# Weight-block differences of the down projection made on GpSimd instead of VectorE

## What is computed

```
hid = conv(h @ w_up)                      # 256 x 11264
gate, up = split(hid)                     # 5632 each
y = (gelu(gate) * up) @ w_down            # 256 x 5632 times 5632 x 2048
```

## Time and profile before

| | before |
|---|---|
| median of 3 runs | 2069.21 us (2067.95 to 2069.44) |
| profiled execution, first to last instruction | 2067.5 us |
| TensorE busy | 2054.3 us, 99% |
| VectorE busy | 1525.8 us, 74% |
| ScalarE busy | 987.2 us, 48% |
| GpSimd busy | 15.5 us, 1% |
| TensorE clock granted | 0.999 of full |

### The profile page before, as it was taken

One profiled execution on the slowest core, in us unless ns is written; L12 is line 12 of the kernel. 1 busy time (PEld: TensorE's weight loads), 2 busy tenths in 40 slices (PEclk: granted clock), 3 DMA queues, 4 the chain that ended last, 5 costly groups with the idle time before them and its releaser, 6 DMA issues.

```text
span 2067.5 us, 26666 instructions
## 1 busy us (share of the span) xinstructions
PE 2054.3 (99%) x10852; PEld 1763.2 (85%) x10852; DVE 1525.8 (74%) x1855; ACT 987.2 (48%) x986; POOL 15.5 (1%) x33
## 2 busy tenths in 40 slices
PE   9999999999999999999999999999999999999999
PEld 7888888888888888878888888888887888888887
DVE  5776786444556767678988887888886778888776
ACT  6444363354434455465544544455454434444642
POOL 0000000000000000000000000000000000000000
PEclk9999999999999999999999999999999999999999
DMA  9756656446566675545665556556566554554463
GB/s 329 223 182 202 176 169 218 150 156 208 159 202 222 241 251 186 181 157 189 204 203 180 192 202 201 183 190 197 195 212 234 172 185 143 183 183 142 144 239 107
DMA packets 296250, 397.68 MB, mean 192 GB/s; under 512 B 16864, under 2 KB 221712, under 8 KB 294464
## 3 DMA queue, kind: packets, MB, share of 16 engines
q1 hardware_dynamic: 292032, 375.02, 55.8%
q0 software_dynamic: 3376, 18.85, 2.5%
q10 hardware_dynamic: 720, 2.11, 0.3%
HBM read 391.76 MB, written 4.19 MB: 192 GB/s over the span
## 4 chain that ended last, share of the span: by engine, by line
PE 96%; DVE 1%; ACT 1%; issue 1%; DMA 1%; SPq 0%; DVEq 0%; ACTq 0%
PE ps L694 89%; PE pm L694 5%; PE pm L697 1%; ACT wh L1258 1%; DVE wl L1845 1%; DMA raw<-in_w_in 0%; DMA xin<-in_x_by_features 0%; ACT xt L1258 0%; DVE up L2023 0%; DVE cv L1853 0%; DVE xt L1853 0%; DVE up L1845 0%; DVE yA L1845 0%; ACT cv L1258 0%; DVE yM L1845 0%
## 5 line engine op out<-in xcount | busy, mean ns | idle before, releaser
L1845 DVE TENSOR_TENSOR wl<-raw,wh 128x2048 fp32r<-128x2048 f32 (+2 forms) x371 | 796.0, 2160 | 288.6 <-ACT wh L1258 208.3
L1258 ACT ACTIVATE wh<-raw 128x2048 fp32r<-128x2048 f32 (+1 forms) x359 | 667.6, 1872 | 319.3 <-PE ps L694 264.4
L694 PE MATMUL ps<-xt,wh 128*128 128x512 f32 (+1 forms) x2752 | 638.9, 388 | 0.2 <-ACT wh L1258 0.2
L694 PEld LDWEIGHTS ps<-xt,wh 128*128 128x128 f32 (+1 forms) x2752 | 505.9, 188 | 101.4 <-issue 1.3
L694 PE MATMUL ps<-wh,xt 128*128 128x512 f32 x1632 | 395.5, 391 | 3.1 <-ACT wh L1258 1.5
L694 PEld LDWEIGHTS ps<-wh,xt 128*128 128x128 f32 x1632 | 303.8, 188 | 67.8 <-issue 2.9
L694 PEld LDWEIGHTS ps<-xt,wl 128*128 128x128 f32 (+1 forms) x2720 | 338.2, 191 | 7.0
L694 PE MATMUL ps<-xt,wl 128*128 128x256 f32 (+1 forms) x2720 | 340.7, 283 | 0.0
L694 PE MATMUL ps<-wl,xt 128*128 128x512 f32 x816 | 207.4, 390 | 0.6 <-DVE wl L1845 0.6
L694 PEld LDWEIGHTS ps<-wl,xt 128*128 128x128 f32 x816 | 152.8, 188 | 33.9 <-DVE wl L1845 2.3
L1258 ACT ACTIVATE cv<-up,vt 128x256 f32<-128x256 f32 x88 | 52.7, 601 | 220.9 <-DVE up L1845 220.9
(11 more groups left out here) (390 smaller groups left out, 1579.9 us busy)
## 6 DMA issues: line engine op xcount, KB each, us to landing
raw<-in_w_in SPq DMA_DIRECT2D x146, 1024.0 KB, 5.4
raw<-in_ffn_w_up SPq DMA_DIRECT2D x84, 1024.0 KB, 5.2
raw<-in_ffn_w_down SPq DMA_DIRECT2D x43, 1024.0 KB, 5.1
raw<-in_w_out SPq DMA_DIRECT2D x32, 1024.0 KB, 5.2
raw<-in_w_proj_b SPq DMA_DIRECT2D x16, 1024.0 KB, 5.3
raw<-in_w_proj_a SPq DMA_DIRECT2D x8, 1024.0 KB, 5.2
raw<-in_xa_wk SPq DMA_DIRECT2D x4, 1024.0 KB, 5.0
raw<-in_xa_wq SPq DMA_DIRECT2D x4, 1024.0 KB, 5.1
```

Of the source, the lines that this page charges most:

```text
L694: return p.matmul(out, l, r, start=start, stop=stop, skip_group_check=share)
L1258: return a.activation(out, in_, func, bias=bias, scale=scale)
L1845: return v.tensor_tensor(out, a, b, op)
```

## The change

The three subtractions leave DVE's list and stand in GpSimd's, in a function `differences` that is called for `dw00` and `dw01` ahead of the transfer of the gain vector, and for `dw10` behind it. GpSimd waits for the landing of `raw`, for the activations, for `s_diffree`, and, between its own three operations, twice for its own result (the second with the new semaphore `s_dift`). DVE keeps its wait for all three and its two `dif_l`. ACT, PE and SP keep their lists; the semaphore `s_dif` counts as before.

```diff
@@ vector_program
         def dif_lo(n):
 
-            half, m, r = int(units[n].g.k_off > 0), seven.index(n), v3(raw[n % 3], 512)
-            d = [v3(dif[half][q], 512) for q in range(2)]
-            v.wait_ge(s_ac, 11 * half + 11)
-            if m:
-                v.wait_ge(s_diffree, m)
-            tt(d[0], bc(r[:, 1:2, :], [128, 2, 512]), r[:, 0:4:3, :], ALU.subtract).then_inc(s_dif, 1)
-            v.wait_ge(s_dif, 2 * m + 1)
-            t = own.add(tt(d[1][:, 0, :], r[:, 0, :], d[0][:, 1, :], ALU.subtract))
-            step(t)
-            tt(d[1][:, 1, :], r[:, 2, :], d[1][:, 0, :], ALU.subtract).then_inc(s_dif, 1)
+            half, m = int(units[n].g.k_off > 0), seven.index(n)
             v.wait_ge(s_dif, 2 * m + 2)
             for q in range(2):
                 v.wait_ge(s_difh, 2 * m + q + 1)
@@ pool_program
+        def differences(name):
+
+            for ui in SEVEN:
+                n = unit_of[name, ui].n
+                half, m, r = int(units[n].g.k_off > 0), seven.index(n), v3(raw[n % 3], 512)
+                d = [v3(dif[half][q], 512) for q in range(2)]
+                e.wait_ge(s_raw[n % 3], raw_count(n))
+                e.wait_ge(s_ac, 11 * half + 11)
+                if m:
+                    e.wait_ge(s_diffree, m)
+                e.tensor_tensor(d[0], bc(r[:, 1:2, :], [128, 2, 512]), r[:, 0:4:3, :], ALU.subtract).then_inc(s_dif, 1)
+                e.wait_ge(s_dif, 2 * m + 1)
+                e.tensor_tensor(d[1][:, 0, :], r[:, 0, :], d[0][:, 1, :], ALU.subtract).then_inc(s_dift, 1)
+                e.wait_ge(s_dift, m + 1)
+                e.tensor_tensor(d[1][:, 1, :], r[:, 2, :], d[1][:, 0, :], ALU.subtract).then_inc(s_dif, 1)
...
+        differences("dw00")
+        differences("dw01")
         e.wait_ge(s_ac, 22)
         e.dma_start(gb3, on_all(I["post_norm_ffn"][0])).then_inc(s_gb3, 16)
 
+        differences("dw10")
```

More of the change, by code:

```diff
@@ L507, in build @@
     s_dif, s_difh, s_difl, s_diffree = sem("dif"), sem("difh"), sem("difl"), sem("diffree")
+    s_dift = sem("dift")
     s_x2out, s_x2in = sem("x2out"), sem("x2in")
```

## The result

The changed kernel takes 2088.62 us (median of 4 runs, 2088.45 to 2090.41), the kernel before 2069.32 us (2067.95 to 2069.78): ratio 1.0098, 95% interval 1.0087 to 1.0110. **It is 19.3 us slower**; forecast were 11.0 us, and the range of 2067.5 to 2088.0 misses it by 0.6 us. The profiled execution is the slowest of the four, span 2088.6 us, 21.1 us over that of before.

What follows compares the result with a forecast made beforehand. TensorE was taken as the bound, with nothing to gain; VectorE and GpSimd excluding each other cost 4.8 (dw00) + 4.8 (dw10) + 1.4 (dw01) = 11.0 us, giving 2080.2 us, range 2067.5 to 2088.

Steps and rivals of the forecast that it cites:

- What bounds the kernel, and that nothing was to gain: Whole kernel and touched pairs: TensorE bounds, busy 2054.3 of 2067.5 us; removing 31.2 us from VectorE is worth 0.
- P: Time of a seven-product unit's three subtractions on GpSimd: between 2.60 and 4.44 us, upper end taken.
- The bound from above: GpSimd's three subtractions costed as an engine taking two inputs in succession, from ScalarE's one-input times: 4.44 us.
- One at a time, in turns: VectorE and GpSimd operations exclude each other whole in dw00, dw01, dw10: 11.0 us lost; rival A, chance 0.62.
- The pair stall: Each further pair in dw00 and dw10 costs P - 2.84 = 1.6 us; 4.8 us per group, dw01 1.4.
- VectorE's sums at the end of a group come a few us later, beside products of the next group: 0: Groups' ends: later VectorE sums were taken to hide beside the next group's products, cost 0.
- a possible gain: Rival D, groups' edges: shorter VectorE lists free one of TensorE's waits, summing to 4.0 us; at best 2065, chance 0.03.
- the ring: Per pair, hops, ScalarE's `dif_h` and `wh`, VectorE's low parts and P: 7.36 + P = 11.80 us against TensorE's 10.20.
- SP's transfer behind each difference ... Cost 0: Transfer starts up to 7 us later than the release, still lands ahead of ScalarE's turn: cost 0.
- The waits behind GpSimd's list: Gain transfer and reload, standing behind GpSimd's added operations: both cost 0.
- Own range of the forecast: Rival A's own range, 2074 to 2088 us; P = 5.5 gives about 19 us.
- 6 (P - 2.84): Loss in dw00 and dw10 as a function of P; dw01 adds something near 1 us.

Runs made afterwards that it cites:

- the dummy operations: Kernel before, plus GpSimd subtractions, copies or constant writes at dw10's four releases that nobody waits for: 2088.61, 2077.57 and 2069.25 us.
- the held-back transfers: Kernel before, with SyncE holding the transfer behind each seven-product unit until TensorE has done that unit's products with the high parts: 2083.35 us, ratio 1.0069.
- The delayed VectorE: Kernel before, with VectorE making the first difference of unit 8 of each wide group three times instead of once: 2074.80 us, ratio 1.0030.
- transfer freed: Changed kernel, with GpSimd's unit 8 differences reading activations and SyncE not waiting for them before the transfer behind unit 8: 2087.33 us, ratio 1.0089.
- the dummy subtractions: Kernel before, plus three GpSimd subtractions of the same sizes at each of dw10's four releases, which nobody waits for: 2088.61 us, ratio 1.0097.
- the low parts cut: Changed kernel, with the low parts of units 9 and 10 of each wide group cut to 8 columns: 2093.77 us, ratio 1.0120.

## Why the prediction was wrong

- **What bounds the kernel, and that nothing was to gain**: right as far as it was tried: with differences a quarter cheaper the kernel is as fast as before, and no run takes them off VectorE altogether without putting them elsewhere.
- **P**: taken as 4.44 us, measured alone 4.98. The bound from above, two one-input passes of ScalarE, was 0.5 us too low. The Trainium skill's figure (GPSIMD Engine Reference, section 3.1), scaled, gave an estimate of the same 4.5 us; the trace has 0.14 to 0.18 us more for each operation, 2.39 and 1.30 where half and a quarter of 4497 ns are 2.25 and 1.12.
- **One at a time, in turns**: right, and shown by the dummy operations. In the turns above the operation that comes second lasts for the rest of the other's time and about its own, on both engines. The trace agrees with the Trainium skill (SBUF — State Buffer, section Who interferes with whom), by which a VectorE instruction with two SBUF inputs contends with a GpSimd instruction that reads SBUF, over a port pair that is locked exclusively. Not wholly exclusive as measured: from 1176.81 to 1182.99 us GpSimd's 4.98 and VectorE's 1.91 us of work pass in 6.18, so some 0.7 us overlap at the changes of turn.
- **The pair stall**: forecast 1.6 us, measured 1.20 (11.40 less 10.20). Three errors of size, one up and two down: P 0.54 us more, the overlap 0.7 us less, and from the last difference to the next `wl` 2.93 us instead of 3.16. In all, dw00 3.65 us (forecast 4.8), dw10 4.2 (4.8), dw01 1.05 (1.4), with its first three pairs free, as forecast. So the pairs came 2.1 us under the forecast, which hides part of the next error: the total misses by 8.3 us only.
- **"VectorE's sums at the end of a group come a few us later, beside products of the next group: 0"**: this is the step that failed: put at 0, measured 11.8 us, of which part is slower products, below. The forecast followed each wait to its next engine inside the pairs and stopped where the pairs end. The rows for it were there. In dw00 the last difference is 7.0 us ahead of unit 9; the sums and evacuation stand in order behind it, and before they waited for TensorE only 0.30 and 1.36 us. In the changed kernel the ring puts the last difference 4.0 us later against TensorE (3.0 us ahead). 4.0 less the slack of 1.66 us is 2.3; TensorE stood 2.2 us between products at 1208 to 1211 (2.6 between loads). At dw10 there was no slack at all: TensorE already waited there for `yA`, 1.8 us. I had read that row as a possible gain and not as a sign of no margin.
- **"SP's transfer behind each difference ... Cost 0"**: right inside the pairs, wrong at the ends, as the held-back transfers and the chain over the end of dw00 show: this term, too, was part of the 11.8 us put at 0.
- **The waits behind GpSimd's list** (gain vector, reload): cost 0, right; the reload still waits 25.0 us for VectorE.
- **Own range of the forecast**, 2074 to 2088: the far end came from larger P alone. A rival "the last difference is late" was missing from the list. By the forecast's own rule 6 (P - 2.84) the P of 4.98 us gives 12.8 us for dw00 and dw10, where 7.85 were lost in their pairs; that 19.3 us lie near the far end of the range is no merit of the rule.

## What the runs showed of the hardware

**Slower products behind a wait.** Behind TensorE's longest waits its products came slower. Behind the wait of 2.2 to 2.6 us at the end of dw00 eight matmuls follow at 0.43 us each instead of 0.23:

```profile
1210.85 0.77 PE L695 MATMUL ps<-wh,ach 128*128 128x512 f32 x1 [2.17 <-DVE yA L1846]
1211.41 0.63 PE L695 MATMUL ps<-wh,acl 128*128 128x512 f32 x1
1211.84 0.63 PE L695 MATMUL ps<-wh,ach 128*128 128x512 f32 x1
```

In that 8 us window the granted clock was 0.79 of full in the mean, and 0.54 from 1585 to 1590 us behind the wait of 4.0 us between products at dw10: close to the lower of its two levels, 1.2 GHz. There ten matmuls from 1585.39 to 1589.74 us take 4.35 us where ten at 0.23 take 2.27. Together some 1.6 us and 2.1 us, a third of what the ends cost and none of it a wait. The delayed VectorE has the same behind dw10: a wait of 2.6 us, then a clock of 0.52 in 5 us. Waits between products of 1.4 us (before, dw10), 1.5 (changed, end of dw01) and 1.7 (transfer freed, end of dw00) left the clock at 1.00, and so did the stalls inside the changed kernel's pairs.

TensorE's busy time on the page grew by 9.7 us. Slower products are some 3.7 of them. Another 4 are the pair stalls, of whose 1.20 us the windows book 0.59 as busy (10.79 against 10.20 us for the same products), if all seven are booked like the one shown. The rest is not accounted for.

**Who pays when two operations meet.** The one that came second is recorded longer, not idle. Inside the pairs VectorE's 128x2048 `wl` comes first and stays at 2.29 us, while its 128x512 operation behind it grew from 0.69 to 2.88 us, in the changed kernel and beside the dummy subtractions alike. Where GpSimd came first, at the end of dw00 with the low parts cut, the 128x2048 one grew as well (6.68 us for two). A mean by form shows this at once, a busy share hides it: VectorE's busy time hardly changed while its work fell by 31 us.

## What to carry to other kernels

An engine's spare time is not free capacity if its operations and its neighbour's hold each other up: add the durations of the two-input operations of VectorE and of GpSimd's reading ones as if on one engine, and compare the sum with the bound's period. Here 6.96 + 4.98 = 11.94 us stood against 10.20, and 11.40 were measured; with the dummy subtractions 9.56 + 4.98 = 14.54, and 13.92 were measured. Only work that falls where the other waits anyway is free, and only if nothing in order behind it comes late. When a ring of engines slips against the bound, follow the slip past the end of the loop, to the first work in order behind it that the bound waits for, and read there how much slack the trace of before shows; a small wait of the bound already standing there means none. A long stall of TensorE should be costed at more than its length: the one of 2.2 us here took 1.6 us more in slower products, the one of 4.0 us 2.1 us more.
